# Two transformer blocks on one core: the modulation and the context work move from a prologue into the two layers

## The reference

```python
# first block, twice
hn = rmsnorm(h, norm1[i]);  z = hn @ w_in[i]          # q, k, v, u
h = h + concat(pool_mixer(u), dilated_mixer(q, k, v)) @ w_out[i]
h = h + square(relu(rmsnorm(h, norm2[i]) @ w_up[i])) @ w_down[i]
h = h + sigmoid(rmsnorm(h, norm3[i]) @ w_gate[i]) * (p[i] @ w_ple[i])
# second block
mod   = silu(c) @ w_mod + b_mod                        # 6 x 1024 numbers, for the latent tokens
mod_c = silu(c_ctx) @ w_mod + b_mod                    # the same weights, for the context
h  = modulate(x, norm1_g, sh1, sc1)
hc = modulate(ctx, norm1_g, csh1, csc1)
# keys and values of the context -> conv, silu, l2norm -> gated delta rule, both directions
# -> a state, from which the delta rule of the latent tokens starts
x = x + g1 * branch_merge(...)
x = x + g2 * swiglu(modulate(x, norm2_g, sh2, sc2), w_ffn_in, w_ffn_out)
```

## Time and profile before

| | |
|---|---|
| times of three executions | 1495.29, 1499.83, 1502.73 us (median 1499.83) |
| the profiled execution | 1494.76 us, span 1493.0 us |
| PE busy | 1354.7 us, 91% of the span |
| weight load on PE, beside the matmuls | 1282.4 us |
| DVE busy | 902.5 us, 60% |
| ACT busy | 701.3 us, 47% |
| POOL busy | 134.1 us, 9% |
| read from HBM | 216.26 MB, 146 GB/s over the span |
| granted TensorE clock, mean | 0.956 of 2.4 GHz |

### The profile page before, as it was taken

How to read it: one execution, slowest core, us unless ns; L and a number is a source line. 1 busy time by engine, 2 the same in 40 slices (tenths; PEclk the granted TensorE clock), 3 DMA queues, 4 the chain that set the end, 5 groups by cost and what they waited for, 6 DMA issues and landing times.

```text
span 1493.0 us, 26105 instructions
## 1 busy us (share of the span) xinstructions
PE 1354.7 (91%) x10476; PEld 1282.4 (86%) x10476; DVE 902.5 (60%) x1265; ACT 701.3 (47%) x1025; POOL 134.1 (9%) x110
## 2 busy tenths in 40 slices
PE   2896889979999988979999998898889999999997
PEld 2775779869999987968999998898778999899997
DVE  2867867755555467675555458756755556554553
ACT  3754544545444445464444445654424454534442
POOL 0025011120000010130000004001520000000000
PEclk9988999989999999979999999899999999999999
DMA  8742634325555553523555544344200555455550
GB/s 298 226 141 86 206 113 142 114 85 167 172 170 182 176 187 105 163 76 114 169 170 184 200 157 138 113 142 142 85 1 29 170 191 166 141 181 189 178 169 29
DMA packets 175843, 219.04 MB, mean 147 GB/s; under 512 B 5001, under 2 KB 159463, under 8 KB 175591
## 3 DMA queue, kind: packets, MB, share of 16 engines
q1 hardware_dynamic: 173986, 212.80, 43.8%
q10 hardware_dynamic: 1732, 4.52, 0.8%
HBM read 216.26 MB, written 1.05 MB: 146 GB/s over the span
## 4 chain that ended last, share of the span: by engine, by line
PE 74%; DVE 12%; DVEq 4%; issue 4%; ACT 3%; DMA 1%; ACTq 0%; SPq 0%
PE bank L629 21%; PE bank L631 20%; PE bank L630 20%; DVE w_lo L620 2%; PE bank L1359 2%; PE bank L870 1%; PE bank L858 1%; DMA w_raw<-in_w_mod 1%; DVE arena L1174 1%; ACT w_hi L611 1%; PE bank L1540 1%; PE bank L1422 1%; DVE arena L2200 1%; PE bank L1341 1%; DVEq L2160 1%
## 5 line engine op out<-in xcount | busy, mean ns | idle before, releaser
L620 DVE TENSOR_TENSOR w_lo<-w_raw,w_hi 128x1024 fp32r<-128x1024 f32 (+1 forms) x406 | 491.5, 1252 | 178.0 <-ACT w_hi L611 170.2
L629 PE MATMUL bank<-act_hi,w_hi 128*128 128x256 f32 x1808 | 522.0, 289 | 29.7 <-DVE act_lo L2123 11.1
L630 PE MATMUL bank<-act_lo,w_hi 128*128 128x256 f32 x1808 | 517.1, 286 | 0.0
L631 PE MATMUL bank<-act_hi,w_lo 128*128 128x256 f32 x1808 | 516.8, 286 | 0.0
L611 ACT ACTIVATE w_hi<-w_raw 128x1024 fp32r<-128x1024 f32 (+1 forms) x406 | 405.0, 1041 | 168.2 <-PE bank L631 112.8
L629 PEld LDWEIGHTS bank<-act_hi,w_hi 128*128 128x128 f32 x1808 | 352.8, 195 | 36.5 <-issue 12.7
L630 PEld LDWEIGHTS bank<-act_lo,w_hi 128*128 128x128 f32 x1808 | 352.8, 195 | 0.3 <-issue 0.2
L631 PEld LDWEIGHTS bank<-act_hi,w_lo 128*128 128x128 f32 x1808 | 352.6, 195 | 0.0
L629 PE MATMUL bank<-side_hi,w_hi 128*128 128x256 f32 x896 | 258.9, 289 | 6.7 <-DVE w_lo L620 6.7
L630 PE MATMUL bank<-side_lo,w_hi 128*128 128x256 f32 x896 | 254.8, 284 | 0.0
L631 PE MATMUL bank<-side_hi,w_lo 128*128 128x256 f32 x896 | 254.8, 284 | 0.0
(11 more groups left out here) (315 smaller groups left out, 1510.2 us busy)
## 6 DMA issues: line engine op xcount, KB each, us to landing
w_raw<-in_w_in SPq DMA_DIRECT2D x40, 1024.0 KB, 5.6
w_raw<-in_w_up SPq DMA_DIRECT2D x32, 1024.0 KB, 5.6
w_raw<-in_w_down SPq DMA_DIRECT2D x32, 1024.0 KB, 5.4
w_raw<-in_w_mod SPq DMA_DIRECT2D x24, 1024.0 KB, 5.2
w_raw<-in_w_ffn_in SPq DMA_DIRECT2D x22, 1024.0 KB, 5.1
w_raw<-in_w_gate SPq DMA_DIRECT2D x20, 1024.0 KB, 5.1
w_raw<-in_w_ffn_out SPq DMA_DIRECT2D x11, 1024.0 KB, 4.9
w_raw<-in_w_out SPq DMA_DIRECT2D x8, 1024.0 KB, 5.0
```

The lines of the kernel that those rows point to most:

```text
L620: nc.vector.tensor_tensor(wlo[:, slot, 0:n], raw[:, l % RAW, n * half:n * (half + 1)], whi[:, slot, 0:n].bitcast(F32), ALU.subtract).then_ ...
L629: nc.tensor.matmul(o, ahi, bhi, start=start, stop=False, skip_group_check=True)
L630: nc.tensor.matmul(o, ahi, blo, start=False, stop=False, skip_group_check=True)
L631: return nc.tensor.matmul(o, alo, bhi, start=False, stop=stop, skip_group_check=True)
```

## The change

The prologue goes. What is left ahead of layer 0 is the small vectors, the rotary tables and the transposition of x.

- **Modulation** is laid out as 12 pairs of chunks, each 512 rows x 512 columns, and isn't split: `mod_chunk` reads the raw slot with four fp32 matmuls of 512 columns, the k-th with 32 stationary columns and its output in partitions 32k to 32k+31 of one bank. Its slot is free when PE has read it (`direct_done`). ACT copies a pair's bank (`modr`), four small matmuls sum the groups (`modc`), DVE adds the bias (`mod_sum`). Chunks 0 to 11 stand in the attention of layer 0, chunks 12 to 23 in its FFN, two for every four chunks of the layer.
- **The context** goes to layer 1. Its transposes stand after chunk 4 (`features_first`), its four projections and its beta/alpha product in the attention, each projection as 16 fp32 matmuls of 256 columns from the raw slot (`project_whole`). Its delta rule begins after the attention, and at 31 places in it one of the chunks 10 to 45 of the layer is multiplied (`fill` calls `step`).
- **The loop** over the layers is unrolled, the copies into `cur_vec` go, and the `n1` input for a next layer (`next_input`) is no longer made in the last layer.
- In the context's delta rule `inverse_x` stands after a further filler, and the scratch that `key_products` reads alternates between two buffers.

```diff
-FILL = {"ctx": dict(norm=2, tok=1, T3=1, z1=1, z2=1, z3=1, z4=1, z5=1, z6=1, x1=1, x2=1, x3=1, x4=1, x5=1, u0=1),
+FILL = {"ctx": dict(ba=1, norm=2, tok=1, T0=1, T1=1, T2=1, T3=1, P=1, x0=1, u1=1, u3=1, s0=1,
+                    **{f"{w}{lv}": 1 for w in "zxt" for lv in range(1, LEVELS)}),
         "lat": dict(ba=2, norm=4, T0=1, T1=1, T2=1, T3=1, end=1)}
...
+ATT_EXTRA = (
+    {"v2": mod(0, 1, 2, 3), 0: [("modr", 0)] + mod(4, 5), 1: [("modr", 1), ("modc", 0)] + mod(6, 7),
+     2: [("modr", 2), ("modc", 1)] + mod(8, 9), 3: [("modr", 3), ("modc", 2)] + mod(10, 11),
+     4: [("modr", 4), ("modc", 3)], 5: [("modr", 5), ("modc", 4)], "V": [("modc", 5)]},
+    {"v2": [("ctx", 0)], 0: [("ctx", 1)], 2: [("ctx", 2)], 3: [("conv", 0)], 4: [("ctx", 3), ("conv", 1)],
+     5: [("conv", 2)], "V": [("conv", 3), ("ba", 0)]})
+FFN_EXTRA = ({}, {})
+for j in range(6, MOD_PAIRS):
+    for at, entry in ((0, ("mod", 2 * j)), (2, ("mod", 2 * j + 1)), (3, ("modr", j)), (4, ("modc", j))):
+        FFN_EXTRA[0].setdefault(16 + 4 * (j - 6) + at, []).append(entry)
...
+            early = 8 if layer == 0 else 3
+            for s in range(LAYER_CHUNKS):
+                if s == 10:
+                    add_direct(direct[:early])
+                if s == 11:
+                    add_direct(direct[early:])
+                st.add((layer, s), src[s], CH // 2 if s in (46, 47) else CH)
+                add_direct(FFN_EXTRA[layer].get(s - 1, []))
...
+        def project_whole(pe, name, bank, act):
+            pe.wait_ge(landed[st.slot(name)], st.loads(name))
+            for m in range(2):
+                for k in range(KT):
+                    at = 256 * k + P * m
+                    mm = nc.tensor.matmul(ps[bank][:, T * m:T * (m + 1)], raw[:, st.slot(name), at:at + P], act[:, k, :],
+                                          start=k == 0, stop=k == KT - 1)
+            mm.then_inc(direct_done, 1)
...
+                for k in range(4):
+                    mm = nc.tensor.matmul(ps[b][32 * k:32 * (k + 1), :], mod_cond[:, 4 * r + k, :],
+                                          raw[:, st.slot(name), 512 * k:512 * (k + 1)], start=r == 0, stop=r == 1,
+                                          skip_group_check=True)
+                mm.then_inc(direct_done, 1)
...
-                    for k in range(4):
-                        f = 4 * half + k
-                        for w in (whi, wlo):
-                            mm = nc.tensor.matmul(o, mod_in[:, f, :], w[:, slot, 256 * k:256 * (k + 1)],
-                                                  start=f == 0 and w is whi, stop=f == KT - 1 and w is wlo)
...
-            with pe.Fori(0, DEPTH) as layer:
+            for layer in range(DEPTH):
...
+                if layer == CTX_LAYER:
+                    pe_delta(pe, "ctx", D_CTX, high, filler("ctx", step))
+                while todo:
+                    step()
...
                 def next_input(c):
-                    norm_lo("n1", LV, range(2 * c, 2 * c + 2), in_hi, in_lo, KT)
+                    if layer + 1 < DEPTH:
+                        norm_lo("n1", LV, range(2 * c, 2 * c + 2), in_hi, in_lo, KT)
...
+            def slot_free(n):
+                if n < RAW:
+                    return
+                before = st.chunks[n - RAW][0]
+                if before in st.split:
+                    sp.wait_ge(lo_ready, st.pieces(before, 1))
+                else:
+                    sp.wait_ge(direct_done, st.direct[before] + 1)
```

More of the change, by code:

```diff
@@ L189, in __init__ @@
         self.full, self.free = full, free
-        self.uses, self.fulls, self.per = {}, {}, {}
+        self.uses, self.fulls = {}, {}
         self.n_use = [0] * 8
         self.n_full = [0] * 8
[L194 to L308, removed]
-    for b in range(3):
-        for c in range(4):
-            lin(f"gate{b}{c}")
-        for c in range(4):
-            lin(f"y{b}{c}")
-    for c in range(4):
-        lin(f"wo{c}")
-    own("norm2")
-    low, high = ring([0, 1, 2, 3]), ring([4, 5, 6, 7])
-    for b in range(4):
-        uses.append((f"ffo{b}", b, 0))
-    for j in range(FF2 // 256):
-        for n in "ab":
-            uses.append((f"ff{n}{j}", high(), 0))
-    uses.append(("final2", 4, 1))
-    for c in range(4):
-        own(f"y_out{c}")
-    banks.section("post", uses)
@@ L383, in heads, with ring, take, filler @@
+def ring(order):
+    n = [0]
+    def take():
+        n[0] += 1
+        return order[(n[0] - 1) % len(order)]
+    return take
+def filler(part, step):
+    left = dict(FILL[part])
+    def fill(point, most=None):
+        n = left.get(point, 0)
+        n = n if most is None else min(n, most)
+        left[point] = left.get(point, 0) - n
+        for _ in range(n):
+            step()
+    return fill
 def heads(b):
@@ L1329, in _ @@
         @block.tensor
         def _(pe):
[L1331 to L1332 removed]
+            full = banks.filled
             tr = lambda o, x: nc.tensor.transpose(o, x, ident)
[L1334 to L1343 removed]
@@ L1410, in ssq @@
+            for layer in range(DEPTH):
+                W = lambda use: banks.wait_full(pe, (layer, use))
+                low, high = ring([0, 1, 2, 3]), ring([4, 5, 6, 7])
+                CL = lambda use: banks.claim(pe, (layer, use), low())
+                C = lambda use: banks.claim(pe, (layer, use), high())
+                wait = lambda name, n, per: pe.wait_ge(S(name), layer * per + n)
+                def ssq(use, n, b):
                     wait("ssq_in", n, 3)
-                    b = C(use)
@@ L1827, in _ @@
+                if layer == CTX_LAYER:
+                    act_delta(act, "ctx", D_CTX, filler("ctx", step))
+                while todo:
+                    step()
+                split_hi(act, chunk(layer, 47))
+                split_hi(act, chunk(layer, 48))
                 for c in range(4):
@@ L2269, in _ @@
+                if layer == CTX_LAYER:
+                    dve_delta(dve, "ctx", D_CTX, filler("ctx", step))
+                while todo:
+                    step()
+                split_lo(dve, chunk(layer, 47))
                 wait("inv_ms", 1, 1)
```

1345 lines of the change are left out of this document (682 added, 663 removed).

## The result

The changed kernel takes 1419.22 us (median of four, 1412.41 to 1422.11) against 1498.93 (1495.29 to 1502.73): ratio 0.9461, 95% interval 0.942 to 0.9503. The forecast was 1408, within 1385 to 1450. The profiled execution took 1418.92 us with a span of 1417.1, 75.9 us less than before; the sum had 88.9.

What follows compares the result with a forecast made beforehand. PE was taken to bound most of the span (busy 91%), DMA the first 25 us. Terms −197.2 + 38.2 + 74.1 − 4 = −88.9 took the span from 1493.0 to 1404; forecast 1408 us, range 1385 to 1450.

Steps and rivals of the forecast that it cites:

- Prologue, −197.2: Before layer 0: the 222.2 us prologue goes, and the first layer matmul starts at 25 us, saving 197.2 us.
- Attention of layer 0, +26.5: Layer 0's attention: modulation loads lengthen it from 24.70 us by 26.5, chunk 11 landing last; bounds 0 and +36.
- FFN of layer 0, +17: Layer 0's FFN: twelve modulation chunks at 0.9 us of PE each, plus copies, sums and tile changes, add 17 us.
- The rival by strict order (2.1): Modulation matmuls start in strict order, 2.1 us a chunk, giving 1425 us; chance 0.15 together with fully serial groups (1446).
- Turn of the loop, −5.3: Between the layers: PE's 3.7 us wait for w_lo and a half-clock chunk of some 1.6 us go, saving 5.3.
- the context's transposes, +1.8: Layer 1 ahead of its attention: 16 transposes of the context at 0.111 us each add 1.8 us.
- Attention of layer 1, +15.5 − 1.8: Layer 1's attention: context projections and beta/alpha product add 15.5 us (bounds +8, +31); 1.8 gained at its now covered end.
- Delta rule, +50.6 + 8: Context's delta rule in layer 1: 50.6 us of PE products plus 8 us of waits over 31 gaps (bounds 0, 48).
- the entry of post, −4: Entry of post: without next_input PE's 3.1 us wait for DVE goes and the clock doesn't fall, saving 4 us.
- The rival of 31 stalls (1572): Layer 1's woven delta rule: each of 31 gaps costs a 3.7 us wait and 1.6 at half clock, +164; chance 0.05.
- The rival that the chain's waits come over whole: Layer 1's woven delta rule: the whole 48 us beside the products come over, +40, so 1448 us; chance 0.18.

Runs made afterwards that it cites:

- e3: Changed kernel with modulation chunk 11 loaded ahead of w_out's first chunk in layer 0's attention: 1415.72 us, ratio 0.9456 to the kernel before.
- e1: Changed kernel with all four matmuls of a modulation chunk in one column group instead of four: 1468.15 us, ratio 0.9797 to the kernel before.
- e9: The changed kernel again, unaltered, on the chip of two later variants: 1420.76 us, ratio 0.9486 to the kernel before.
- e7: Changed kernel with key_products ahead of the filler, the FFN norm's sum of squares later, and POOL's three delta-rule products on DVE: 1410.55 us, ratio 0.9419.
- e2: Changed kernel with DVE forming key_products ahead of the filler chunk in the context's delta rule: 1415.26 us, ratio 0.945 to the kernel before.
- e5: Changed kernel with the context's delta rule in one piece, no layer chunks multiplied between its steps: 1445.49 us, ratio 0.9652 to the kernel before.

## Why the prediction was right, and where its sizes were off

The mechanism held in the main, with luck in three of the terms, and the time lies 11 us above the forecast. The sum gave a span of 1404; it was 1417.1, 13 us more. (From its 1406 us for an execution and the factor 1.0034 the prediction makes a median of 1411 and then states 1408, without a reason.) By the terms of the sum:

- *Prologue, −197.2:* measured −197.9, the first matmul at 24.31 us, forecast 25. Part of that is luck: the vectors land later than I had it (9.9 us, not 7), and the rest takes 14.4 us instead of 18. The terms as listed add up to 21.0 us and not to 21.5.
- *Attention of layer 0, +26.5:* measured +25.1, and 1.4 ahead of it. Chunk 11 was issued 31.7 us and landed 37.1 us after the projection's end; the prediction had 32 and 37.6. These numbers came out by luck. The loads were faster than taken: they ran at 383 GB/s for 20 us, `w_out`'s first chunk was in 18.6 us after the projection's end and modulation 10 after 26.7, where the prediction has both in at 29.5. What then held chunk 11 back until 32 was DVE's list, which the prediction doesn't have. And e3 showed that this last load, which I took for the end of the stage, has another wait right behind it.
- *FFN of layer 0, +17:* measured +18.1. A chunk cost 1.0 us instead of the 0.9 taken. The rival by strict order (2.1) falls. The page "TensorE: Matmul & The Clock Gate" of the Trainium skill, Part 3, has three column tiles at 2.38x, 0.79 of three; here four gave 3.55 / 1.0 = 3.5x (e1), 0.89 of four. Its strict order of starts, from which the prediction estimated five passes, doesn't show in the cost: the trace has the first entries of all four matmuls within 0.02 us of each other, from 194.42 on, and the second entries from 194.87 on.
- *Turn of the loop, −5.3, and the context's transposes, +1.8:* measured −3.4 for both, forecast −3.5. The turn's second wait went; the first (2.99 us before) is still there at 2.68, and a wait of 2.0 for the transposes is new. The agreement is luck: in e9's trace of the same kernel the stretch took 82.2 us instead of 79.4, a gain of 0.6, at a lower clock. Also, DVE did not spend 3.3 us in vector copies at the turn: the row is idle time ahead of a copy of 0.18.
- *Attention of layer 1, +15.5 − 1.8:* measured +20.4, 6.7 more. The four projections were right (27.7 against 27.6). I had used layer 0's 24.7 us for a stage that took 23.0 here, and had counted the end's wait as gained although it lay in those 23.0. The beta and alpha product took 5.1 us, not 3.6, at a granted clock of 0.69; in e7 the same 32 instructions took 3.6 at 1.00. The rest is T and V, 10.4 us on PE instead of some 9. The +15.5 was PE's own work at full clock with every wait hidden, so it was a lower bound (the stated +8 lies below it and can't be reached), and taking 1.8 off it left no way to be right.
- *Delta rule, +50.6 + 8, and the entry of post, −4:* measured +61.7 in all, 7.1 more than the 54.6. The products took 49.5 us. The waits of the weave were 12.8 instead of 8, in two places; e2 removes both, and others come. In return the FFN's own waits fell by some 4. The entry of post gave 2.5 instead of 4: PE no longer waits 3.1 for DVE's `next_input`, but 4.6 us (2.9 before) for POOL, which squares the third quarter of the input. And 6.2 us, not in the sum, lie in the layer's own matmuls: the same 1969 took 247.5 us from start to start, waits left out, instead of 241.3. Of these, 3.5 are matmuls at half clock: 9 and 16 of them behind the two large waits and 16 behind the beta and alpha product, 1.5 us for 16. Another 3.0 are the first matmul behind each piece of the delta rule, which holds PE some 0.2 us instead of 0.12. I had counted the slow stretch behind a wait at the loop's turn, and not in the weave.

So the whole miss lies in layer 1: its three stretches grew by 78.7 us (372.3 to 451.0), where the sum has 64.8. Two terms were sized too low. The attention took PE's least possible work for the time, and the delta rule lacked what PE's own matmuls lose beside each wait and each change of work. The rival of 31 stalls (1572) falls, as PE waited for `w_lo` in one gap only. The rival that the chain's waits come over whole falls too: 12.8 us of waits, where the bare chain has 22 and a lower clock (e5), and not the 48 that it took.

## What to carry to other kernels

A prologue that needs only loads and a chain of small products can go into stages that have other things to spare, but ask of each stage what it can spare: loads went best where PE is full, products where PE is idle, and the same eight chunks cost 22 us in the gap and some 11 in the full stage. When work is woven into another engine's list, look for the operation that frees a buffer or lets a load start and stands behind the filler: it made the large waits here, in the weave and in layer 0's attention. Price a wait with the slow matmuls behind it, up to 1.5 us here, and each change of work with some 0.1 us. And where a term is the busiest engine's own work, it is the least that the stage can take: put the forecast above it.

## What the runs showed of the hardware

- Four fp32 matmuls with 32 stationary columns each, in four column groups, take 1.0 us for 512 columns, against 3.55 us in one group.
- DVE and POOL slow each other in some operations. DVE's subtraction of 128x1024 takes 1.18 us alone and 2.3 beside POOL's products (e2). POOL's product with a constant takes 1.26 us alone (e5, 574.25) and 2.09 beside DVE's subtraction (e2, 590.10); its addition took 1.27 beside it (e2, 588.68).
- The granted clock falls at some places in some executions and not in others: 0.69 in the beta and alpha product of the changed kernel, 1.00 for the same instructions in e7, with PE busy throughout in both and a DMA share of 1.08 and 1.09. It makes 3 us with the chunk behind it. The stretch ahead of layer 1's attention took 79.4 and 82.2 us in two traces of the changed kernel. PE got its first vectors between 7.2 and 11.0 us in the traces of the changed kernel and its variants. The nine executions of the changed kernel spread over 11 us (1412.41 to 1423.82); how much of that each of these makes is not shown.
- In layer 0's attention loads ran at 383 GB/s for 20 us (104 to 124), faster than the 323 of the burst before.
